# A hybrid block stack with attention and experts on one core: order of work in the layers, an earlier start of the heads, a split output projection

## What is computed

```
hybrid layer (twice):
  h      = rms_norm(x) * (1 + scale) + shift;  proj = h @ w_in
  o_pool = (window mean of u over 2, 4, 8, 16 tokens - u) @ pool_w * silu(gate)
  o_ret  = chunked retention, 4 heads of 128, chunks of 128 tokens:
           o_n = (q k^T * decay) v + q_dec R_n;  R_(n+1) = chunk_decay R_n + k_tail^T v
  o_rwkv = RWKV-7 time mixing, 8 heads of 64: head norm * ln_w + ln_b + bonus
  x      = x + gate * (sum of sigmoid gates * (branch @ w_branch)) @ w_out
attention layer:
  q, k, v of 8 dilated heads and of 8 forgetting heads = rms_norm(x) @ w_in
  o_dil, o_fox = softmax(q k^T + bias) v;  each is rms-normed over its 512 features
  x      = x + concat(o_dil, o_fox) @ w_out
experts:  32, top-1 of 4 groups, top-2 in the group, SwiGLU; then a final rms_norm
```

## Time and profile before

| | |
|---|---|
| median of 3 runs | 2028.56 us (2026.48 to 2032.41) |
| profiled execution | 2035.46 us, span of its trace 2033.0 us |
| mean granted TensorE clock | 0.964 of full |
| TensorE busy | 1921.1 us, 94% of the span |
| VectorE busy | 1137.3 us, 56% |
| ScalarE busy | 761.0 us, 37% |
| GpSimd busy | 692.8 us, 34% |

### The profile page before, as it was taken

How to read it: one execution, slowest core, us unless ns; L and a number is a source line. 1 busy time by engine, 2 the same in 40 slices (tenths; PEclk the granted TensorE clock), 3 DMA queues, 4 the chain that set the end, 5 groups by cost and what they waited for, 6 DMA issues and landing times. The chain is left out here.

```text
span 2033.0 us, 26274 instructions
## 1 busy us (share of the span) xinstructions
PE 1921.1 (94%) x10768; PEld 1550.0 (76%) x10768; DVE 1137.3 (56%) x1425; ACT 761.0 (37%) x1121; POOL 692.8 (34%) x391
## 2 busy tenths in 40 slices
PE   8998999999999899999999999989989889999994
PEld 6777899988888777889998888869868775555552
DVE  5258755556665418765546677432145346666664
ACT  3346210333223343511233222343356544555552
POOL 0349210424444346721142444434400112333330
PEclk7999999999999899999999999989979889999997
DMA  7222300214544322220122554334200068999983
GB/s 313 94 83 76 111 1 11 85 61 174 174 173 143 115 93 93 80 77 1 43 84 80 201 176 169 101 124 166 94 20 1 32 262 313 346 341 337 337 280 133
DMA packets 78142, 284.56 MB, mean 140 GB/s; under 512 B 27283, under 2 KB 27411, under 8 KB 60740
## 3 DMA queue, kind: packets, MB, share of 16 engines
q1 hardware_dynamic: 71140, 272.29, 38.4%
q0 software_dynamic: 6144, 8.40, 1.2%
q10 hardware_dynamic: 736, 2.14, 0.3%
HBM read 274.37 MB, written 23.63 MB: 147 GB/s over the span
## 5 line engine op out<-in xcount | busy, mean ns | idle before, releaser
L1508 POOL TENSOR_TENSOR wmem_r<-wmem,wmem_r 128x1024 fp32r<-128x1024 f32 x170 | 419.6, 2469 | 658.4 <-ACT wmem_r L1024 647.4
L693 PE MATMUL banks<-h_hi_r,wmem_r 128*128 128x512 f32 x1632 | 514.1, 394 | 13.5 <-POOL wmem_r L1508 7.5
L693 PEld LDWEIGHTS banks<-h_hi_r,wmem_r 128*128 128x128 f32 x1632 | 310.0, 190 | 82.3 <-POOL wmem_r L1508 9.4
L1024 ACT ACTIVATE wmem_r<-wmem 128x1024 fp32r<-128x1024 f32 x170 | 180.2, 1060 | 488.9 <-DMA wmem<-wstream 486.2
L693 PE MATMUL banks<-hT_r,wmem_r 128*128 128x512 f32 x816 | 320.6, 393 | 0.0
L693 PEld LDWEIGHTS banks<-hT_r,wmem_r 128*128 128x128 f32 x816 | 155.0, 190 | 32.3 <-issue 0.5
L2076 PE MATMUL banks<-wmem_r,gm_mem_r 128*80 128x512 f32 x496 | 178.2, 420 | 0.0
L2604 POOL TENSOR_TENSOR wmem_r<-wmem,wmem_r 128x1024 fp32r<-128x1024 f32 x30 | 74.8, 2493 | 234.5 <-ACT wmem_r L2144 234.5
L1748 POOL DMA_INDIRECT y_tok_dram<-ztp,y_idx x32 | 66.4, 2074 | 226.2 <-DVE ztp L2530 218.8
L714 PE MATMUL banks<-wmem_r,h_hi_r 128*128 128x256 f32 x768 | 140.3, 286 | 0.0
L1448 DVE SCALAR_TENSOR_TENSOR ztp<-xT,c_act,ztp 128x256 f32<-128x256 f32 x168 | 129.1, 768 | 6.0
(11 more groups left out here) (424 smaller groups left out, 3318.6 us busy)
## 6 DMA issues: line engine op xcount, KB each, us to landing
wmem<-wstream SPq DMA_DIRECT2D x206, 512.0 KB, 3.7
slots<-experts SPq DMA_DIRECT2D x80, 1024.0 KB, 7.4
xT<-ada SPq DMA_DIRECT2D x24, 1024.0 KB, 5.9
xT<-experts SPq DMA_DIRECT2D x16, 1024.0 KB, 7.4
slots<-ada SPq DMA_DIRECT2D x8, 1024.0 KB, 17.7
x_keep<-xT SPq DMA_DIRECT2D x2, 2048.0 KB, 17.8
xT<-x_keep SPq DMA_DIRECT2D x2, 2048.0 KB, 8.4
dil_rows<-dil_once SPq DMA_DIRECT2D x1, 2560.0 KB
```

The source lines that it names most:

```text
L693: mm = nc.tensor.matmul(o, r(lhs[:, k, :]), r(rhs[:, k, :]), start=(k == 0 and i == 0), stop=(k == KD - 1 and i == 2))
L1024: inc(nc.scalar.activation(r(chunk(b)[0]), w, ACT.Copy), "w_high")
L1508: inc(g.tensor_tensor(r(lo), lo, r(hi), ALU.subtract), "w_split")
```

## The change

- *Layers, ScalarE:* the rounding behind the last k copy is issued after the four decay sigmoids.
- *Layers, GpSimd:* window sums are made in two buffers with 8 zero columns ahead, so that the prefix copies go (one remains, of one column). The calls of `low` and the windows come in another order.
- *Layers, retention:* kv comes before the output in the list; the output's four products without state are issued ahead of the wait for the state, the four with it behind. VectorE waits for the output to be complete before it updates the state.
- *Layers, VectorE:* the four `ln_w` scalings first, then the four `ln_b` steps.
- *Entry into the heads:* scores 0 and 1 are issued behind the first block of the last value projection (vf), scores 2 and turn 0 in the middle of its second block. ScalarE does the exponentials of pairs 0 to 2 and `turned(0)` before it copies the last two vf banks. Scores then run three pairs ahead of the values. The first three score tiles lie in another buffer. Forgetting pairs wait for all 24 copies, dilated ones for the first 8 and 12. The roundings of chunks OUT to OUT+2 move from the vf copies to pairs 5, 7 and 9.
- *In the heads:* the first kind's square root (ScalarE, pair 22), reciprocal and four row scalings (VectorE, pairs 24 and 25), transposes `ot0` to `ot3` (TensorE, after pairs 25 and 27), copies and roundings (ScalarE, pairs 27 to 30), subtractions (VectorE).
- *After the heads:* the second kind's square root in two parts, row scalings on VectorE; `ao0` and `ao1` run their first halves (features of the first kind) at once, then `ot4` to `ot7`, then the second halves. ScalarE writes only the rounded part of `ot4` to `ot7`; VectorE subtracts it from the scaled PSUM bank.

The work is the same otherwise. The diff, cut:

```diff
         for n in range(NT):
             if n < NT - 1:
                 job(f"sc{n + 1}", "pret_ready", 2 + n)
+                job(f"kv{n}", "R_ready", 1 + n)
             job(f"o{n}", "o_ready", 1 + n)
...
-                after("pret_ready", n + 1)
                 if n == 0:
                     after("ret_tok")
-                else:
-                    after("R_ready", n)
...
+                head = [slice(h * P, h * P + P) for h in range(RET_H)]
                 if n < NT - 1:
                     o = open_bank(f"kv{n}")
+                    for cols in head:
+                        mm = nc.tensor.matmul(o[:, cols], k_tail[:, n, cols], rv_tok[:, n, cols], start=True, stop=True)
                     full(mm)
+                after("pret_ready", n + 1)
+                o = open_bank(f"o{n}")
+                for h, cols in enumerate(head):
+                    mm = nc.tensor.matmul(o[:, cols], p_ret[n % 2][:, cols], rv_tok[:, n, cols],
+                                          start=(h == 0), stop=(n == 0), skip_group_check=True)
+                if n > 0:
+                    after("R_ready", n)
+                    for h, cols in enumerate(head):
+                        mm = nc.tensor.matmul(o[:, cols], qdT[:, h, t0:t0 + P], state[:, h, :],
+                                              start=False, stop=True, skip_group_check=True)
+                full(mm)
...
+                    if (name, c) != ("k", CW - 1):
+                        high(FIRST[name] + c + RING)
                 if name == "k":
                     for c in range(CW):
                         inc(nc.scalar.activation(G_[:, c, :], bank(f"z{c}"), ACT.Sigmoid, bias=par("w0", c)), "g_ready")
+                    high(FIRST["k"] + CW - 1 + RING)
...
+                    after("bank_full", FULL[f"o{n}"])
...
-                step(v.scalar_tensor_tensor(br_rwkv[:, c, :], bank(f"ty{c}"), par("ln_w", c), br_rwkv[:, c, :], ALU.mult, ALU.add),
-                     "y_scaled")
+                inc(v.scalar_tensor_tensor(br_rwkv[:, c, :], bank(f"ty{c}"), par("ln_w", c), br_rwkv[:, c, :], ALU.mult, ALU.add),
+                    "y_scaled")
+            for c in range(CW):
+                after("y_scaled", c + 1)
                 inc(v.scalar_tensor_tensor(br_rwkv[:, c, :], br_rwkv[:, c, :], par("ln_b", c), rg_gate[:, c, :], ALU.add, ALU.mult),
                     "rwkv_done")
...
+            PAD = max(WINDOWS) // 2
+            padded = [flat_ztp[:, i * (PAD + T):(i + 1) * (PAD + T)] for i in range(2)]
+            fix = flat_ztp[:, 2 * (PAD + T):2 * (PAD + T) + 16]
+            summed = {}
+
+            def window_sums(i):
+
+                u = pool_u[:, i, :]
+                after("pu_ready", i + 1)
+                dst, other = padded
+                inc(g.tensor_copy(dst[:, PAD:PAD + 1], u[:, 0:1]), "pool_step")
+                count[0] += 1
+                step(g.tensor_tensor(dst[:, PAD + 1:], u[:, 1:T], u[:, 0:T - 1], ALU.add))
+                lag = 2
+                while lag < WINDOWS[i]:
+                    step(g.tensor_tensor(other[:, PAD:], dst[:, PAD:], dst[:, PAD - lag:PAD - lag + T], ALU.add))
+                    dst, other, lag = other, dst, 2 * lag
+                summed[i] = dst[:, PAD:]
+
+            def window_rest(i):
+
+                u, src = pool_u[:, i, :], summed[i]
+                inc(g.tensor_tensor(fix, src[:, 0:16], con("inv_count")[:, 16 * i:16 * i + 16], ALU.mult), "pool_step")
+                count[0] += 1
+                step(g.tensor_scalar(src[:, 16:], src[:, 16:], 1.0 / WINDOWS[i], None, ALU.mult))
+                step(g.tensor_tensor(u[:, 16:], src[:, 16:], u[:, 16:], ALU.subtract))
+                inc(g.tensor_tensor(u[:, 0:16], fix, u[:, 0:16], ALU.subtract), "pool_d")
...
+            for a in padded:
+                inc(g.memset(a[:, 0:PAD], 0.0), "pool_step")
+                count[0] += 1
+            low(FIRST["pg"], FIRST["pg"] + 1)
+            window_sums(0)
+            low(FIRST["pg"] + 1, FIRST["pg"] + 2)
+            window_rest(0)
+            low(FIRST["pg"] + 2, FIRST["rg"])
+            window_sums(1)
+            window_rest(1)
+            window_sums(2)
+            window_rest(2)
+            low(FIRST["rg"], FIRST["rg"] + 2)
+            window_sums(3)
+            window_rest(3)
+            low(FIRST["rg"] + 2, FIRST["tg"])
...
+        AHEAD = 3
+        FIRST_TURNS = {6 * PER_GRP + 1: (0, 1), 6 * PER_GRP + 3: (2, 3)}
         for i, what in enumerate(("qd", "kd", "vd", "qf", "kf", "vf")):
             for c in range(CW):
+                if what == "vf" and c == 2:
+                    assert len(jobs) % 2 == 0
+                    for k in range(AHEAD - 1):
+                        for e in range(2):
+                            job(f"s{k}{e}", "s_shifted", k + 1)
                 job(f"{what}{c}", "qkv_ready", 4 * i + c + 1)
-        pairs = [(kind, tb, h) for kind in range(2) for tb in range(NT) for h in range(0, DIL_H, 2)]
-        PER_GRP = DIL_H // 2
-        assert len(jobs) % 2 == 0
-        for i in range(-2, len(pairs)):
+        for i in range(-1, len(pairs)):
...
+                            if what == "vf" and (b, half) == (1, 0):
+                                scores(AHEAD - 1)
+                                turn(0)
+                        if what == "vf" and b == 0:
+                            after("qkv_ready", 8)
+                            for k in range(AHEAD - 1):
+                                scores(k)
+
+                after("qkv_ready", 12)
...
+                def out_part(w, o, kind):
+
+                    for k in range(kind * CW, kind * CW + CW):
+                        after("oT_split", CW if kind == 0 else k + 1)
+                        for i, (lhs, rhs) in enumerate(((w[0], h_hi[:, k, :]), (w[0], o_low[k]), (w[1], h_hi[:, k, :]))):
+                            mm = nc.tensor.matmul(o, r(lhs[:, k, :]), r(rhs), start=(k == 0 and i == 0), stop=(k == KD - 1 and i == 2))
+                    return mm
...
+                for i in range(len(pairs)):
+                    if i + AHEAD < len(pairs):
+                        if pairs[i + AHEAD][0] == 1:
+                            after("qkv_ready", 24)
+                        scores(i + AHEAD)
+                    if i + 1 < len(pairs):
+                        turn(i + 1)
+                    values(i)
+                    for c in FIRST_TURNS.get(i, ()):
+                        turn_out(c)
+
+                o = [open_bank(f"ao{c}") for c in range(2)]
+                for c in range(2):
+                    out_part(out_weights(c), o[c], 0)
+                for c in range(CW, KD):
+                    turn_out(c)
...
-                    feature_job(f"ao{c}", OUT + c, (h_hi, oT), fresh=(c == 0))
+                    if c >= 2:
+                        o = open_bank(f"ao{c}")
+                        out_part(out_weights(c), o, 0)
+                    full(out_part(out_weights(c), o if c >= 2 else o[c], 1))
...
+                        if what == "vf" and c == 2:
+                            for k in range(AHEAD):
+                                exps(k)
+                            turned(0)
...
+                def tile_roots(first, end):
+
+                    nc.scalar.activation(hvar[:, first:end], hvar[:, first:end], ACT.Sqrt, bias=con("eps")).then_inc(SEM["o_root"], 1)
+
+                def out_high(c):
+
+                    if c < CW:
+                        nc.scalar.activation(r(h_hi[:, c, :]), o_low[c], ACT.Copy).then_inc(SEM["oT_high"], 1)
+                    else:
+                        nc.scalar.activation(r(h_hi[:, c, :]), bank(f"ot{c}"), ACT.Copy, scale=glob("out_norm", c)).then_inc(SEM["oT_high"], 1)
+
+                def out_copy(c):
+
+                    nc.scalar.activation(o_low[c], bank(f"ot{c}"), ACT.Copy, scale=glob("out_norm", c)).then_inc(SEM["oT_ready"], 1)
...
+                    if i in OUT_HIGHS:
+                        high(OUT + OUT_HIGHS.index(i))
+                    if i == ROOT_AT:
+                        after("o_sq", NT)
+                        tile_roots(0, NT)
+                    for c in FIRST_TURNS.get(i - 2, ()):
+                        out_copy(c)
+                    for c in FIRST_TURNS.get(i - 3, ()):
+                        after("oT_ready", c + 1)
+                        out_high(c)
...
+                after("o_sq", 2 * NT)
+                tile_roots(2 * NT - 1, 2 * NT)
+                for c in range(CW, KD):
+                    out_high(c)
...
+                def out_low(c):
+
+                    after("oT_high", c + 1)
+                    if c < CW:
+                        ins = v.tensor_tensor(r(o_low[c]), o_low[c], r(h_hi[:, c, :]), ALU.subtract)
+                    else:
+                        ins = v.scalar_tensor_tensor(r(o_low[c]), bank(f"ot{c}"), glob("out_norm", c), r(h_hi[:, c, :]), ALU.mult, ALU.subtract)
+                    ins.then_inc(SEM["oT_split"], 1)
...
```

(10 more changed lines are left out.)

224 lines of the change are left out of this document (97 added, 127 removed).

## The result

The changed kernel takes 2000.48 us (median of 4, 2000.01 to 2003.15) where the kernel before took 2030.49 beside it (2026.48 to 2037.49): 30.0 us less, ratio 0.9851 with a 95% interval of 0.9821 to 0.9881. The forecast was 1997.0, the range 1984 to 2008.

What follows compares the result with a forecast made beforehand. TensorE, busy 94% of the span, was taken as the bound, so time could be won only where it stands or runs at low clock. 9.4 + 13.5 - 3.3 + 11.8 = 31.4 off 2028.56 gave 1997.2, stated as 1997.0; range 1984 to 2008.

Steps and rivals of the forecast that it cites:

- sigmoids first: Layers, before the first value projection: TensorE's wait for the decay sigmoid's bank goes, with low clock in layer 0; 4.3 us gained.
- pool sums: Layers, GpSimd's windows: TensorE's 7 us per layer mostly spent standing before the relative scores; net 0, range -5 to +6.
- retention order: Layers, last retention chunk: TensorE's stand for the state VectorE updates is covered; 1.0 us per layer, 2.0 gained.
- scales first: Layers: TensorE's 1.54 us stand for the fourth ln_w scaling goes in both layers; 3.1 us gained.
- entry into the heads: Behind the last value projection: work of 29.99 us takes 16.5 if the clock stays up; 13.5 us gained.
- in the heads: Attention heads: added transposes cost TensorE 1.8 us and stalls 1.5 (0 to 6); 3.3 us lost.
- out of the heads: Heads to third output job: half jobs cover the steps to the row scaling; 18.6 us against 30.43, 11.8 gained.
- rival (b): Layers: VectorE is not the bound of the relative-score job, so 7.2 us per layer is kept; 1983 us; chance 0.11.
- One sign of being right: Layers: no TensorE wait for the pool-gate subtraction, but a pause of 4 us or more before the second relative-score half.
- Rival (a): Entry: heads start at low clock although the pause is gone; gain 6 us for 13.5, 2004.5 us; chance 0.20.

Runs made afterwards that it cites:

- old_pool: The changed kernel with GpSimd's pool part as it was before (prefix copies, old order of subtractions); 2000.16 us.
- entry_late: The changed kernel with scores 2 and turn 0 behind the last value projection and the first three pairs of exponentials behind its copies; 2011.15 us.
- no_root: The changed kernel with the early square root of the first kind (pair 22) left out and a copy in its place; 2000.54 us.
- layers_only: The kernel before with the layer edits alone, the attention part as before; 2020.98 us, ratio 0.9950.

## Why the prediction was right, and which steps were off

| step | said, us | the traces, us |
|---|---|---|
| sigmoids first | 4.3 | 1.4 + 1.5 of clock + 1.4: 4.3 |
| pool sums | 0 | -3.2 against the kernel before; 0.1 with the old code put back |
| retention order | 2.0 | 3.0 (1.5 per layer) |
| scales first | 3.1 | 3.6 |
| entry into the heads | 13.5 | 13.9 |
| in the heads | -3.3 | -4.2 |
| out of the heads | 11.8 | 11.6 (30.43 to 18.81) |
| sum | 31.4 | 29.0; 30.6 with the stages that no edit touches; 30.0 between medians |

Each term was read from one pause and the one behind it, and most came out that way. That the sum was within 1.4 us of the measured gain is in part luck: the pool sums and the stalls in the heads cost 4.1 us more than I had put down, and retention, scales and two falls of the clock that did not come gave 3.8 back. Term by term:

*Sigmoids first* and *scales first* went as worked out; scales gained the 1.54 us and 0.25 more. The 1.5 of clock shows in VectorE's chain: its reciprocal starts 35.19 us behind the start of the value projection, where it started 36.73 behind it.

*Retention order* was mis-sized: I counted the last chunk alone. The earlier chunks gained as well, 0.2 to 0.4 us each.

*Pool sums.* The step that the gain of 7 us per layer would be spent standing held, and it is the reading with the largest consequence: rival (b) had 14 us more, and `old_pool` excludes it. The size 0 did not hold against the kernel before. There the low clock came at 166 us, ahead of the wait for the bonus products, so that the work it delayed only shortened that wait. Now it comes behind the last wait: from the second half of the relative scores to the gates TensorE takes 9.7 us for 7.5 in layer 0 and 9.6 for 7.6 in layer 1. VectorE's chain from the reciprocal to the bonus products became only 0.3 and 0.8 us shorter. That makes -3.2. I had set 2.5 of low clock against 2.6 of chain; over both layers it was 4.2 against 1.1. `old_pool` gives 0.1 all the same, because its clock is low behind the last wait as well (from 184.2 us on), which it wasn't in the kernel before. Two details were off. I put the scans 2.6 us sooner; they ended 1.2 us sooner once the 1.2 of the sigmoids are taken off, and the three products behind them, which I had not laid beside the new list, took 9.3 us for 8.4. And there are two stands, 2.24 before the first half of the relative scores and 4.30 before the second; I had only the second. One sign of being right failed too: TensorE still waits 0.90 and 0.95 us for the subtraction of a pool-gate chunk, where I had written that no such wait would be left.

*Entry.* Worked out from jobs at full clock, it came to 0.4 us. Rival (a), low clock although the pause is gone, did not come: the clock is 1.00, with stands of 0.78, 1.21 and 1.26 us left in the first 30. That the term hangs on the clock was right: in `entry_late`, where the pause is back, 6 us of it are lost to the low clock.

*In the heads.* About 1.9 us are the transposes; the stalls are 2.3 us, not 1.5. I had taken the two table switches as mostly hidden in ScalarE's 31 us of idle time. They came at a point where an exponential was due, and 1.4 us of them got through. Idle time summed over a stretch doesn't hide a lump of 2.9 us. VectorE has a part too: two turns or scores that wait for its bias step stand 1.40 and 1.49 us, where they stood 0.61 and 0.66 before, and `no_root` leaves both as they are. Ahead of the first of them VectorE now has two row scalings (0.88 us); what delays the second wasn't tried.

*Out of the heads.* The chain of about 3 us did fit under the 5.45 us of first halves; the wait behind the transposes is 0.35 for my 0.5.

*Not forecast* were differences that no edit is shown to have made: in the changed trace the clock doesn't fall at 344 us (1.5 us) and is low for less long at the start of layer 1 (0.8), and the experts differ by 6.4.

## What to carry to other kernels

Before a wait is priced, ask what the engine behind the next one does: a stand that ends on another engine's serial chain only moves. Put work of a second kind across a chain of small steps (the half jobs over the root), since a covered pause saves its length and the low clock behind it. And when a stretch is shortened, read the next three stages too: here 4 to 5 us per layer won at the relative scores were lost again, in four of the five kernels that tried, to a late subtraction, a late inverse and a clock that fell elsewhere. A median of four executions that differ by 3 to 13 us doesn't settle 2 us, and one trace of the fastest of them doesn't either.

## What the runs showed of the hardware

- VectorE and GpSimd exclude each other for whole two-input instructions, both ways: 2.29 became 4.37 us beside 2.58 of GpSimd, and GpSimd's 2.4 became 4.43. VectorE's reciprocal, which has one input, wasn't touched: 12.95 us with GpSimd busy for 7.50 of them, 12.94 with it busy for 12.54.
- The low clock isn't tied to the length of a pause alone. Behind the same pause of 0.78 us at about 340 us the clock was 1.00 in the changed kernel and seven others, and 0.77 to 0.89 in six: the kernel before, `old_pool`, and the four with the bonus products first. It costs 1.5 to 3.4 us in a layer. When the clock was last low does not decide it: in `old_pool` and in `layers_only` it was last low up to 187.6 us and the pause came at 338.9, and it fell in the first (0.89 from 335 to 350 us) and not in the second (1.00). Why the same pause does the one or the other, no run here shows.
- Pauses of 2.07 and 0.69 us before small jobs left 0.72 of full clock over 30 us; one of 2.04, with 0.78 about 4 us before it and 0.76 about 7 us behind it, left 0.94.
